# SSD decay rows and the samples' x*dt rows copied to all partitions by DMA instead of by TensorE products, and the samples' steps moved into the next group's steps

## The reference, cut to what matters

```python
acum = jnp.cumsum(dt * a, axis=2)
seg = jnp.exp(jnp.where(causal, acum[:, :, :, None] - acum[:, :, None], -jnp.inf))
xdt = x * dt[..., None]
cb = jnp.einsum('bctgn,bcsgn->bctsg', cm, bm)
y_diag = jnp.einsum('bctsg,bctsgh,bcsghp->bctghp', cb, seg, xdt)
chunk_states = jnp.einsum('bcsgn,bcsgh,bcsghp->bcghpn', bm, decay_to_end, xdt)
y_off = jnp.einsum('bctgn,bcghpn,bctgh->bctghp', cm, s_in, jnp.exp(acum))
```

## Time and profile before

| what | value |
|---|---|
| median of three runs | 2650.25 us |
| the profiled execution's own time | 2654.2 us |
| its span in the profile | 2652.2 us |
| mean granted TensorE clock | 0.947 of 2.4 GHz |
| PE, DVE, ACT, POOL busy, share of the span | 82%, 57%, 36%, 25% |
| the SSD stage | about 65 to 430 us of the span |

### The profile page before, as it was taken

How to read it: one execution, slowest core, us unless ns; L and a number is a source line. 1 busy time by engine, 2 the same in 40 slices (tenths; PEclk the granted TensorE clock), 3 DMA queues, 4 the chain that set the end, 5 groups by cost and what they waited for, 6 DMA issues and landing times.

```text
span 2652.2 us, 28143 instructions
## 1 busy us (share of the span) xinstructions
PE 2183.6 (82%) x10057; PEld 1426.1 (54%) x10072; DVE 1522.5 (57%) x3214; ACT 950.4 (36%) x2438; POOL 651.8 (25%) x628
## 2 busy tenths in 40 slices
PE   5889887888797998988899988997777777777776
PEld 4868654766497997988644444443322222222222
DVE  3566673233347546543466666666677666666664
ACT  2545432222144344431333333333333433333333
POOL 0101220111100000000144444444434433443431
PEclk7999997899698999999899999999999999999999
DMA  2312312122153653562699999999999999999996
GB/s 74 111 56 76 116 68 73 40 66 66 60 149 114 183 159 108 165 197 91 236 422 421 421 420 419 411 421 421 421 421 421 421 421 421 422 421 421 421 421 263
DMA packets 200190, 693.44 MB, mean 261 GB/s; under 512 B 17537, under 2 KB 113345, under 8 KB 131314
## 3 DMA queue, kind: packets, MB, share of 16 engines
q0 software_dynamic: 74880, 545.29, 49.5%
q1 hardware_dynamic: 125170, 146.35, 17.4%
HBM read 670.71 MB, written 20.81 MB: 261 GB/s over the span
## 4 chain that ended last, share of the span: by engine, by line
DMA 31%; PE 14%; DVE 2%; ACT 2%; issue 1%; POOL 1%; ACTq 0%; POOLq 0%
DMA p_rows<-in_experts,p_idx 31%; PE bank L1931 10%; PE bank L1891 4%; DVE p_rows L1786 2%; ACT p_diag L1838 1%; PE bank L1901 1%; POOL p_rows L1653 1%; ACT p_weight L1831 1%; ACT p_gel L1828 0%; DVE p_x1b L1765 0%; ACT L1850 0%; ACT p_sc L1817 0%; ACT p_q L1810 0%; DVE p_x1b L1756 0%; ACT L1828 0%
## 5 line engine op out<-in xcount | busy, mean ns | idle before, releaser
L1931 PE MATMUL bank<-p_rows,p_diag 128*128 128x512 f32 (+1 forms) x1664 | 779.7, 615 | 198.8 <-ACT p_diag L1838 198.7
L1653 POOL DMA_INDIRECT p_rows<-in_experts,p_idx x416 | 442.1, 1063 | 1226.2 <-DVE p_tv L1683 608.5
L1786 DVE CUSTOM_DVE_ANT_0 p_rows<-p_rows,p_hnb 128x1024 f32<-128x1024 f32 x416 | 510.0, 1226 | 360.5 <-DMA p_rows<-in_experts,p_idx 360.4
L1931 PEld LDWEIGHTS bank<-p_rows,p_diag 128*128 128x128 f32 (+1 forms) x1664 | 308.7, 193 | 651.0 <-issue 330.7
L160 PE MATMUL bank<-x_hi,w_hi 128*128 128x264 f32 (+2 forms) x1152 | 346.7, 301 | 58.6 <-DVE w_lo L154 53.6
L154 DVE TENSOR_TENSOR w_lo<-raw_w,w_hi 128x1024 fp32r<-128x1024 f32 x176 | 218.9, 1244 | 234.8 <-ACT w_hi L146 234.5
L1828 ACT ACTIVATE p_gel<-p_hid 128x2 f32<-128x2 f32 x260 | 52.9, 204 | 827.1 <-DVE p_hid L1786 827.1
L161 PE MATMUL bank<-x_lo,w_hi 128*128 128x264 f32 (+2 forms) x1152 | 335.9, 292 | 0.0
L162 PE MATMUL bank<-x_hi,w_lo 128*128 128x264 f32 (+2 forms) x1152 | 334.8, 291 | 0.0
L160 PEld LDWEIGHTS bank<-x_hi,w_hi 128*128 128x128 f32 x1152 | 225.5, 196 | 66.6 <-DVE w_lo L154 51.4
L146 ACT CAST w_hi<-raw_w 128x1024 fp32r<-128x1024 f32 x176 | 184.0, 1046 | 136.7 <-PE bank L162 136.7
(11 more groups left out here) (357 smaller groups left out, 3096.5 us busy)
## 6 DMA issues: line engine op xcount, KB each, us to landing
raw_w<-in_w_merge SPq DMA_DIRECT2D x80, 512.0 KB, 3.6
raw_w<-in_w_z SPq DMA_DIRECT2D x32, 512.0 KB, 4.2
raw_w<-in_w_ssd SPq DMA_DIRECT2D x24, 512.0 KB, 4.8
s_sst<-in_state_ssd SPq DMA_DIRECT2D x4, 2048.0 KB, 8.9
o_sssd<-s_sst SPq DMA_DIRECT2D x16, 512.0 KB, 2.6
raw_w<-in_w_gla SPq DMA_DIRECT2D x16, 512.0 KB, 4.6
raw_w<-in_w_g SPq DMA_DIRECT2D x16, 512.0 KB, 4.3
query_w<-in_w_query SPq DMA_DIRECT2D x8, 1024.0 KB, 9.2
```

Source lines behind the costliest of these rows:

```text
L1653: nc.gpsimd.indirect_dma_start(row_of(row), None, k.dram["experts"], bass.IndirectOffsetOnAxis(idx[:, slot:slot + 1], 0)).then_inc(row_her ...
L1786: nc.vector.tensor_tensor_reduce(out=u, in0=u, in1=hn, scale=1.0, scalar=0.0, op0=ALU.mult, op1=ALU.add, accum_out=hid[:, n % 2, s:s + 1]) ...
L1931: last = nc.tensor.matmul(ps[b][0:width, :], diag[:, slot % DIAGS, 0:width], row_of(row)[:, D + half * 512:D + half * 512 + 512], start=s ...
```

## The change

It has three parts.

1. **Decay rows.** In the norm stage PE makes the cumulative sums once more in transposed form, DVE copies them out and SP writes them to a scratch array in DRAM (64 KB). In the SSD stage SP reads 4 KB (8 heads by 128) of it to each of the 128 partitions with one DMA per chunk, into one of three `mix` buffers. ACT then makes min(acum[t] - acum[s], 0) with a Relu for each head and one exponential over four heads, and DVE multiplies the B-by-C product by the triangle before it is used. All L478 and L481 products, their semaphore and two constants go.
2. **The samples' rows.** The split into bf16 parts and the L562 products go. SP writes x*dt of 8 samples to DRAM and reads one 2 KB row to all partitions per sample, with two buffers.
3. **Order.** The `sample` entry is replaced by eight `samp` entries, two in each of the next group's four steps, behind `late` and ahead of the tile; the last group's eight stand at the end. The states are loaded and stored in pairs, and POOL's decays move to `sprep`.

```diff
@@ stage_norm @@
+            sp.wait_ge(arow_done, 1)
+            sp.dma_start(k.arow_dram.rearrange("c h t -> h c t"), arow[:, :, :]).then_inc(k.arow_out, 16)
...
-            nc.vector.tensor_scalar(k.nac[:, :, :], ac[:, 0:TILES, :], -1.0, None, ALU.mult)
+            nc.vector.tensor_copy(k.acum[:, :, :], ac[:, 0:TILES, :])
...
+            dve.wait_ge(rows_done, 1)
+            nc.vector.tensor_copy(arow[:, :, :], ps[7][0:HEADS, :].rearrange("h (c t) -> h c t", c=TILES)).then_inc(arow_done, 1)
...
+            for c in range(TILES):
+                last = nc.tensor.matmul(ps[7][0:HEADS, c * P:(c + 1) * P], k.da[:, c, :], k.tri[:, :], start=True, stop=True)
+            last.then_inc(rows_done, 1)
@@ ssd_order @@
             order += [("off", g, i - 1), ("front", g, i), ("back", g, i - 1), ("late", g, i)]
+            if g >= 1:
+                order += [("samp", g - 1, 2 * i - 2), ("samp", g - 1, 2 * i - 1)]
             order += tiles[i:i + 1] if i < STEPS - 1 else [("sprep", g, 0)] + tiles[i:]
-        order += [("off", g, STEPS - 1), ("back", g, STEPS - 1), ("sample", g, 0)]
-    return order
+        order += [("off", g, STEPS - 1), ("back", g, STEPS - 1)]
+    return order + [("samp", GROUPS - 1, b) for b in range(NSAMP)]
@@ stage_ssd, sync @@
+            def states(g, pair):
+                two = slice(2 * pair, 2 * pair + 2)
                 if g >= 1:
-                    sp.wait_ge(sst_out, 16 * NSAMP // 2 * g)
-                    sp.wait_ge(sy_ready, g)
+                    sp.wait_ge(sst_out[pair], 16 * g)
+                    sp.wait_ge(sst_read, NSAMP * (g - 1) + 2 * pair + 2)
+                sp.dma_start(sst[:, two, :], k.dram["state_ssd"][g, :, two, :]).then_inc(sst_here[pair], 16)
+            def rows(d):
...
+                if d >= MIXES:
+                    sp.wait_ge(yd_ready, d - MIXES + 1)
+                g, c = divmod(d, TILES)
+                src = k.arow_dram[c, g * HPG:(g + 1) * HPG, :].rearrange("h t -> (h t)").unsqueeze(0).to_broadcast([P, HPG * P])
+                sp.dma_start(mix[:, d % MIXES, :, :, :].rearrange("p a h t -> p (a h t)"), src).then_inc(rows_here[d % MIXES], 16)
+            def spread(q):
+                g, b = divmod(q, NSAMP)
+                if q >= SPREADS:
+                    sp.wait_ge(sst_done, q - SPREADS + 1)
+                sp.dma_start(sxb[:, q % SPREADS, :], k.sx_dram[g, b, :].unsqueeze(0).to_broadcast([P, GW])).then_inc(sxb_here[q % SPREADS], 16)
+            for pair in range(NSAMP // 2):
+                states(0, pair)
+            sp.wait_ge(k.arow_out, 16)
+            for d in range(MIXES - 1):
+                rows(d)
...
+                elif kind == "late":
+                    rows(g * TILES + i + 1)
+                elif kind == "sprep":
+                    if g >= 1:
+                        states(g, NSAMP // 2 - 1)
+                    sp.wait_ge(sxdt_done, g + 1)
+                    sp.dma_start(k.sx_dram[g], sxdt[:, :]).then_inc(sx_out, 16)
+                    sp.wait_ge(sx_out, 16 * (g + 1))
+                    for b in range(SPREADS):
+                        spread(g * NSAMP + b)
+                elif kind == "samp":
+                    if i + SPREADS < NSAMP:
+                        spread(g * NSAMP + i + SPREADS)
+                    if i % 2:
+                        sp.wait_ge(sst_done, NSAMP * g + i + 1)
+                        sp.dma_start(k.dram["o_sssd"][g, :, i - 1:i + 1, :], sst[:, i - 1:i + 1, :]).then_inc(sst_out[i // 2], 16)
+                        if g + 1 < GROUPS and i >= 3:
+                            states(g + 1, i // 2 - 1)
@@ stage_ssd, tensor @@
-                nc.tensor.matmul(ps[SEG][:, :], k.identb[:, :], k.future[:, :], start=True, stop=False)
-                for h in range(4):
-                    hh = g * HPG + half * 4 + h
-                    last = nc.tensor.matmul(ps[SEG][:, h * P:(h + 1) * P], k.da[:, i - 1, hh:hh + 1].to_broadcast([P, P]),
-                                            k.tri[:, :], start=False, stop=h == 3)
...
+                elif kind == "samp":
+                    if i == 0:
+                        pe.wait_ge(cmask_done, g + 1)
+                        if g >= 1:
+                            pe.wait_ge(sy_done, g)
+                    pe.wait_ge(sst_done, g * NSAMP + i + 1)
+                    last = nc.tensor.matmul(ps[SY][0:NSAMP, :], cmask[:, i, :], sst[:, i, :], start=i == 0, stop=i == NSAMP - 1)
+                    last.then_inc(sst_read, 1)
@@ stage_ssd, scalar @@
+                act.wait_ge(rows_here[d % MIXES], 16 * (d // MIXES + 1))
+                v = mix[:, d % MIXES, half, :, :]
                 for h in range(4):
                     hh = g * HPG + half * 4 + h
-                    last = nc.scalar.activation(mix[:, d % 2, half, h, :], ps[SEG][:, h * P:(h + 1) * P], ACT.Exp,
-                                                bias=k.nac[:, i - 1, hh:hh + 1])
-                last.then_inc(exp_done, 1)
+                    last = nc.scalar.activation(v[:, h, :], v[:, h, :], ACT.Relu, scale=-1.0, bias=k.acum[:, i - 1, hh:hh + 1])
+                k.alink(act, last)
+                nc.scalar.activation(v, v, ACT.Exp, scale=-1.0).then_inc(exp_done, 1)
@@ stage_ssd, vector @@
+                        dve.wait_ge(bc_copied, s + 1)
+                        if d >= 1:
+                            dve.wait_ge(mix_done, 2 * d)
+                        nc.vector.tensor_tensor(bcb[:, par, 1, :], ps[BC][:, P:2 * P], k.tri[:, :], ALU.mult).then_inc(cb_done, 1)
                         mix_half(s, d, 0)
...
+                elif kind == "samp":
+                    q = g * NSAMP + i
+                    dve.wait_ge(sdec_done, q + 1)
+                    dve.wait_ge(sxb_here[q % SPREADS], 16 * (q // SPREADS + 1))
+                    nc.vector.scalar_tensor_tensor(sst[:, i, :], sxb[:, q % SPREADS, :], sxc[:, g % 2, B_TILE, i:i + 1],
+                                                   sst[:, i, :], ALU.mult, ALU.add).then_inc(sst_done, 1)
@@ stage_ssd, gpsimd @@
-                elif kind == "front" and i == 1:
-                    pool.wait_ge(sst_here, 16 * (g + 1))
+                elif kind == "sprep":
                     for b in range(NSAMP):
+                        pool.wait_ge(sst_here[b // 2], 16 * (g + 1))
```

More of the change, by code:

```diff
@@ L421, in stage_ssd @@
         xt_ready, bc_ready, xt_used, bc_copied, yoff_done = map(sem, ("xt_ready", "bc_ready", "xt_used", "bc_copied", "yoff_done"))
-        seg_ready, exp_done, mix_done, yd_ready, yo_ready = map(sem, ("seg_ready", "exp_done", "mix_done", "yd_ready", "yo_ready"))
+        exp_done, mix_done, yd_ready, yo_ready, cb_done = map(sem, ("exp_done", "mix_done", "yd_ready", "yo_ready", "cb_done"))
+        rows_here = [sem(f"rows_here{j}") for j in range(MIXES)]
+        sxb_here = [sem(f"sxb_here{j}") for j in range(SPREADS)]
+        sst_here, sst_out = ([sem(f"sst_{what}{j}") for j in range(NSAMP // 2)] for what in ("here", "out"))
+        sx_out = sem("sx_out")
         cs_ready, y_done, state_done, xdt_done, xdec_done, zeroed = map(
@@ L455, in _ @@
                     load_piece(sp, k, g * CT + i + PIECE_BUFS - 1)
-                elif kind == "sample":
-                    for b in range(0, NSAMP, 2):
-                        sp.wait_ge(sst_done, NSAMP * g + b + 2)
-                        sp.dma_start(k.dram["o_sssd"][g, :, b:b + 2, :], sst[:, b:b + 2, :]).then_inc(sst_out, 16)
+                elif kind == "late":
[8 more added lines that the diff above has]
+                        spread(g * NSAMP + b)
+                elif kind == "back" and i == STEPS - 1:
                     sp.wait_ge(state_done, STEPS * (g + 1))
                     sp.dma_start(k.dram["o_pssd"][g], state[:, g % 2, :]).then_inc(pst_out, 16)
-                    if g + 1 < GROUPS:
-                        states(g + 1)
+                elif kind == "samp":
[6 more added lines that the diff above has]
+                            states(g + 1, i // 2 - 1)
             sp.wait_ge(tile_evac, GROUPS * CT)
@@ L467, in _ @@
             sp.wait_ge(conv_out, 32)
-            sp.wait_ge(sst_out, 16 * NSAMP // 2 * GROUPS)
+            for pair in range(NSAMP // 2):
+                sp.wait_ge(sst_out[pair], 16 * GROUPS)
             sp.wait_ge(pst_out, 16 * GROUPS)
@@ L472, in _ @@
         def _(pe):
-            def decays(g, i, half):
-                q = 2 * (g * TILES + i - 1) + half
-                if q >= 1:
-                    pe.wait_ge(exp_done, q)
-                nc.tensor.matmul(ps[SEG][:, :], k.identb[:, :], k.future[:, :], start=True, stop=False)
-                for h in range(4):
-                    hh = g * HPG + half * 4 + h
-                    last = nc.tensor.matmul(ps[SEG][:, h * P:(h + 1) * P], k.da[:, i - 1, hh:hh + 1].to_broadcast([P, P]),
-                                            k.tri[:, :], start=False, stop=h == 3)
-                last.then_inc(seg_ready, 1)
             for kind, g, i in SSD_ORDER:
@@ L502, in _ @@
```

(9 more changed lines are left out.)

85 lines of the change are left out of this document (31 added, 54 removed).

## The result

The changed kernel takes **2688.36 us** (median of 4 runs, 2681.35 to 2690.74) against 2652.04 for the kernel before (4 runs, 2643.74 to 2654.35): ratio **1.0138**, 95% interval 1.0109 to 1.0168, slower by 36 us. 2676 was forecast, with 2653 to 2700 as its range. The profiled execution has a span of 2686.3 us at a mean granted clock of 0.932 (before: 2652.2 and 0.947), so the spans are 34.1 us apart.

The account below looks back on a forecast made before the run. PE and DVE waiting for each other bound the SSD stage (busy 66 and 55 of 75 us). Terms 1 - 21.3 + 3 x 15.5 = +26.2 on 2654.2 gave 2680.4, less 4 to the median: 2676 us, range 2653 to 2700.

Parts of the forecast that it names:

- group 0: SSD stage's first group, no samples added to its steps: shorter steps and boundary, -21.3 us in all.
- group 1: SSD stage: four steps lose 7.3, 8.2, 8.2, 7.5 us, tile 5 gains 1.0, boundary 14.7; +15.5 us.
- group 2: SSD stage: the same terms as group 1, +15.5 us.
- group 3: SSD stage's last group, no tiles, DVE and PE alternate: longer steps and DMA waits, +15.5 us, bounds +11 to +26.
- The loss per step: Groups 1 and 2: PE's sample products wait for DVE's updates, delaying the tile 5.3 to 6.2 us, plus 2.0 for clock.
- E: The moment at which a tile leaves PSUM; times within a step are counted in us from it.
- The gain at the boundaries: From tile 5's departure to the next group's tile 0: 13.3 us instead of 28.03, -14.7, three times.
- The last eight updates: End of group 3: updates wait for spreads by DMA, priced at 2.6 us per landing; 11.2 us in all, 11.6 before.
- SP's queue: At sprep the next group's weight piece lands near 5 us after tile 4's departure and just fits; no cost.
- Rival B: PE's sample products in groups 1 and 2 find updates done: steps of 13.9 us, whole -49, 2601 us; chance 0.10.
- Rival C: SP becomes the bound: landings of 4.8 us instead of 2.6 delay weight pieces; +59, 2709 us; chance 0.12.
- Its second form: ACT: Relu and exponential in different tables, two loads of 1.28 us per half, 2 us per step in group 0.

Follow-up runs that it names:

- fill_wait: The changed kernel with 40 overwritten filler products ahead of each pair of PE's sample products in groups 1 and 2; 1.0092 of before, 2668.2 us.
- rows_only: The kernel before with only the decay rows by DMA (part 1), samples as before; 0.9982 of before, 2638.9 us.
- all_behind: pe_behind_tile with step 4's sample products behind the tile too, a second mask buffer, samples' sum and last state load moved; 0.9878 of before, 2610.4 us.
- updates_first: The changed kernel with DVE's two sample updates ahead of front instead of behind late; 0.9912 of before, 2620.4 us.
- pe_behind_tile: The changed kernel with PE's two sample products behind the tile in steps 1 to 3, other engines' order kept; 0.9897 of before, 2615.5 us.
- rows_fill: rows_only with ten filler products (sixteen in step 4) ahead of the chunk state product; 0.9969 of before, 2638.4 us.
- all_behind_fill: all_behind with ten filler products (sixteen in step 4) ahead of each step's chunk state product; 0.9889 of before, 2616.2 us.
- lump: The changed kernel without the new order: a group's eight samples stand together at its end, as before; 1.0051 of before, 2659.6 us.

## Why the prediction was right, and which terms were off

The mechanism was the forecast one, in direction and in place: PE's sample products wait for updates that stand last in DVE's step, and the tile stands behind them. The terms, by the ends of the stretches:

| term | forecast | measured |
|---|---|---|
| start, with tile 0 | +1 | +1.3 |
| group 0 | -21.3 | -23.3 |
| group 1 | +15.5 | +16.0 |
| group 2 | +15.5 | +14.6 |
| group 3 | +15.5 | +23.0 |
| end of the stage | 0 | -0.7 |

- **The loss per step** was 7.3, 8.2, 8.2, 7.5 by forecast, 8.1, 8.1, 7.7, 8.2 in group 1 and 7.2, 7.5, 8.9, 7.3 in group 2. The products were to start at E+11.4, and 200.39 + 11.4 = 211.8 is where they stand. The clock's share was taken as 2.0 per step, all eight times; fill_wait gave back 1.4, and with its overrun counted about 2.1. The Trainium skill, "TensorE: Matmul & The Clock Gate", section "HAM oscillation — how this bites in real kernels", has such a loop pay for each round and not once. The trace agrees: behind each of the eight waits the four passes take 3.3 to 3.6 us, where they take 1.88 at full clock.
- **The gain at the boundaries**, 14.7 by forecast, was 16.3 and 14.1. **Tile 5** gained 1.9 twice (forecast 0.6 and 1.0), for it no longer waits for its low part.
- **Group 0:** step 1 gained 3.5 (forecast 3.1) and steps 2 and 3 1.6 each (1.4). Step 4 lost 1.5 where a gain of 0.1 was counted, since the clock fell behind the wait of 1.40 us there: the chunk state product ran at half clock (2.07 us), and `sprep`'s transposes behind it, after a further wait of 1.14, did too. The forecast let a wait take the place of a product at no cost; rows_only shows that it isn't free: there the same wait of 1.40 brings the clock down in steps 2 and 3 as well, and part 1 by itself is worth 4 us and not 18.
- **Group 3 is the mis-sized term**, +23.0 instead of +15.5. yoff 1 came as forecast (12.8 us after the group's first transposes, forecast 13). Its steps then took 12.8, 13.1 and 12.8 us, not 11, 11 and 12:

```profile
394.75 0.69 DVE L714 TENSOR_TENSOR s_yoff<-bank,eac 128x512 f32<-128x512 f32 x1 [4.03 <-PE bank L561]
...
401.40 1.41 DVE L748 SCALAR_TENSOR_TENSOR s_sst<-s_sxb,s_sxc,s_sst 128x512 f32<-128x512 f32 x2
407.52 0.69 DVE L714 TENSOR_TENSOR s_yoff<-bank,eac 128x512 f32<-128x512 f32 x1 [4.72 <-PE bank L561]
```

```profile
402.20 3.58 PE L593 MATMUL bank<-s_sst,s_cmask 128*8 128x512 f32 x4 [4.07 <-DVE s_sst L748]
405.71 1.78 PE L561 MATMUL bank<-s_state,s_xc 128*128 128x512 f32 x2
```

  DVE needs 8.05 us (394.75 to 402.8), near the 7.9 counted. But PE then runs all four passes and the state product at half clock, so that yoff comes 4.7 us behind the last update, where 2 to 4 was the range and about 3 was taken. That is somewhat beyond the slow end which the prediction had named for a step. The whole, +23.0, is within its bound of +26 for the group and just beyond the +22 that its range was added up from.
- **The last eight updates** took 15.4 us instead of 11.2. All but the second wait for their spread, the first 1.79 us where 2.7 was counted:

```profile
DVE s_sst L748 <- DMA s_sxb<-sx_kept: 11.1, 7, 3.0
```

  The spread was priced by the nearest row, a store of 512 KB in 2.6 us. It landed in 3.9, and that store itself now takes 4.9; in rows_only, which reads the decay rows but has no spreads, the store keeps its 2.6. A fuller queue is not all of it: the first spreads of group 3 were issued at 435.62, with no weight piece beside them, and DVE could use the first at 439.28, 3.7 us later. The error is in taking another transfer's duration for that of a spread; why a spread takes longer is open.
- **SP's queue:** the weight piece at `sprep` was to fit just so. In the changed kernel it did (tile 5's step 5.9 us), but only because the step before was 22 us long; in all_behind, with a step of 14.5, it was late by 6.05.
- **Rival B** (its own terms add up to -47, not -49), faster because the products find their updates done, did not happen, but updates_first and pe_behind_tile made it true by hand. They gave 23 and 28 us below before, not the 49 that it stated, because step 4 (pe_behind_tile) or a wait of 1 to 3 us (updates_first) remained. **Rival C** fell: the weights landed in 6.3 us and the end of the stage moved by 31, not 59. Its second form did not come either: no table load stands ahead of the Relus (L614).

What stays open: the cause of the 3.2 us between the end of the SSD stage and the end of the kernel, and what decides whether the clock falls behind a stand of 1.4 to 1.9 us. What more than two buffers for the spreads would bring is not known either.

## What to carry to other kernels

When work is moved from a serial stretch into a pipelined loop, its place in each engine's own list matters as much as its cost: the consumer (here PE's sample products) belongs behind the work that does not need it, as late as the producer's place in the other list. The same moved work cost 36 us in one order and saved 28 in another. After that look for the next queue in line, here SP's, where a wait for one small store held the weights of the next tile.

And compare stages by their own ends, not by the whole time: the clock that a later, unchanged stage is granted moved the whole by as much as a real gain.

## What was not expected of the hardware

- **The clock can fall behind much shorter stands than 4.88 us.** In rows_only a stand of 1.40 us was followed by 0.50; in the changed kernel the same 1.40 us left full speed in steps 2 and 3 of group 0 (steps of 11.8 us) and was followed by 0.50 in step 4 and in step 2 of group 1. In the GLA stage the same stand of 1.92 us had either outcome with the same code (0.50 in rows_fill, 1.00 in rows_only), worth 2.9 us a batch and up to 10 us over the stage.
- **Filler products do raise the clock** (0.80 to 0.93 over 75 us in fill_wait), but in the steps of groups 1 and 2 where it was full already they made the steps 1.2 to 1.3 us longer (all_behind_fill).
- **DVE ran slower while POOL computed.** In rows_only the split of a weight piece took 2.06 us instead of 1.22 and three taps 3.15 instead of 2.38, where POOL was at work on the samples (busy until 211.3):

```profile
206.00:210.00 4.00, 2.41 (x16) 1.81 (x16) 4.00 (x4) 3.83 (x9) 4.00 (x4) 1.00 0.00 0
210.00:214.00 4.00, 1.29 (x12) 1.15 (x11) 3.93 (x5) 3.97 (x11) 1.34 (x1) 1.00 0.43 115
```

```profile
208.38 2.06 DVE L154 TENSOR_TENSOR w_lo<-raw_w,w_hi 128x1024 fp32r<-128x1024 f32 x1
210.36 3.15 DVE L670 SCALAR_TENSOR_TENSOR s_cv<-s_raw,s_cw,s_cv 128x528 f32<-128x528 f32 x3
```

  The kernel before has the same: its splits at 211.43 and 299.93 take 2.06 us, with POOL busy from 205.66 to 216.4 and from 294.24 to 304.9, and those outside these times 1.22 or 1.23 from group 1 on. In lump, where POOL had ended its decays at 204.3, the same split took 1.22:

```profile
213.06 1.22 DVE L154 TENSOR_TENSOR w_lo<-raw_w,w_hi 128x1024 fp32r<-128x1024 f32 x1
```

  No kernel was made to try POOL's work by itself.
